# Stick-breaking attention, key block by key block with both heads of a pair side by side

## What is computed

```python
q, k, v, gate = jnp.split(h @ w_in, 4, axis=-1)
q = rms_norm(q.reshape(Bn, T, 16, 64), q_norm_g)
k = rms_norm(k.reshape(Bn, T, 16, 64), k_norm_g)
...
z = jnp.einsum('bqhd,bshd->bhqs', q_blk, k) * scale
mask = key_pos[None, :] < q_pos[:, None]
log1m = jnp.where(mask, -softplus(z), 0.0)
after = cumsum(log1m, axis=3, reverse=True) - log1m
wts = jnp.where(mask, exp(log_sigmoid(z) + after), 0.0)
o = jnp.einsum('bhqs,bshd->bqhd', wts, v)
...
return (o * silu(gate)) @ w_out
```

## Time and profile of the kernel before

| | us |
|---|---|
| time, median of 3 runs (2142.62 to 2148.38) | 2144.33 |
| span of the profiled execution | 2145.8 |
| stick-breaking pairs in it, first `z` to the projection of the gate | 730.3 to 974.9 |

### The profile page before, as it was taken

One profiled execution on the slowest core, in us unless ns is written; L12 is line 12 of the kernel. 1 busy time (PEld: TensorE's weight loads), 2 busy tenths in 40 slices (PEclk: granted clock), 3 DMA queues, 4 the chain that ended last, 5 costly groups with the idle time before them and its releaser, 6 DMA issues.

```text
span 2145.8 us, 28611 instructions
## 1 busy us (share of the span) xinstructions
PE 2056.1 (96%) x10624; PEld 1679.0 (78%) x10624; DVE 1039.1 (48%) x1426; ACT 809.6 (38%) x1169; POOL 619.7 (29%) x156
## 2 busy tenths in 40 slices
PE   6999899999998999999999999999899999999999
PEld 4777788887888766657878888888687788887787
DVE  7856655545424134442564343422874655554620
ACT  5223232237523366563432222222423322234831
POOL 3434000004443210112434444444343300001342
PEclk9999999999999999999999999999999999999999
DMA  4222000002222110111222222222222200000222
GB/s 164 93 98 79 20 1 0 0 0 83 95 98 99 59 40 20 39 39 51 89 96 98 98 95 91 93 92 98 99 98 79 79 1 0 0 0 21 97 98 79
DMA packets 20371, 138.36 MB, mean 64 GB/s; under 512 B 2256, under 2 KB 2384, under 8 KB 4176
## 3 DMA queue, kind: packets, MB, share of 16 engines
q1 hardware_dynamic: 20304, 137.45, 18.2%
HBM read 135.35 MB, written 2.10 MB: 64 GB/s over the span
## 4 chain that ended last, share of the span: by engine, by line
PE 90%; DVE 6%; issue 2%; ACT 1%; POOL 0%; ACTq 0%; DVEq 0%; POOLq 0%
PE ps L1261 20%; PE ps L1263 20%; PE ps L1262 20%; PE ps L1475 4%; PE ps L1459 4%; PE ps L1640 2%; PE ps L1678 2%; PE ps L1666 1%; PE ps L1541 1%; PE ps L1493 1%; PE ps L1522 1%; DVE inv_t L1016 1%; PE ps L1534 1%; PE ps L1523 1%; PE ps L1484 1%
## 5 line engine op out<-in xcount | busy, mean ns | idle before, releaser
L294 POOL TENSOR_TENSOR w_lo<-w_raw,w_hi 128x2048 fp32r<-128x2048 f32 x126 | 589.4, 4678 | 1117.0 <-ACT w_hi L354 1117.0
L1261 PE MATMUL ps<-h_hi,w_hi 128*128 128x512 f32 x1488 | 597.9, 402 | 34.2 <-POOL w_lo L294 20.5
L1262 PE MATMUL ps<-h_lo,w_hi 128*128 128x512 f32 x1488 | 584.1, 393 | 0.0
L1263 PE MATMUL ps<-h_hi,w_lo 128*128 128x512 f32 x1488 | 584.0, 392 | 0.0
L1261 PEld LDWEIGHTS ps<-h_hi,w_hi 128*128 128x128 f32 x1488 | 283.0, 190 | 107.7 <-POOL w_lo L294 21.4
L354 ACT ACTIVATE w_hi<-w_raw 128x2048 fp32r<-128x2048 f32 x126 | 240.4, 1908 | 271.7 <-PE ps L1263 267.2
L1262 PEld LDWEIGHTS ps<-h_lo,w_hi 128*128 128x128 f32 x1488 | 282.8, 190 | 62.3 <-issue 5.1
L1263 PEld LDWEIGHTS ps<-h_hi,w_lo 128*128 128x128 f32 x1488 | 282.1, 190 | 60.1
L1261 PE MATMUL ps<-y_hi,w_hi 128*128 128x512 f32 x448 | 174.3, 389 | 0.0
L1262 PE MATMUL ps<-y_lo,w_hi 128*128 128x512 f32 x448 | 174.3, 389 | 0.0
L1263 PE MATMUL ps<-y_hi,w_lo 128*128 128x512 f32 x448 | 174.3, 389 | 0.0
(11 more groups left out here) (181 smaller groups left out, 2753.1 us busy)
## 6 DMA issues: line engine op xcount, KB each, us to landing
w_raw<-w_tiles SPq DMA_DIRECT2D x126, 1024.0 KB, 4.8
x<-x_t SPq DMA_DIRECT2D x4, 512.0 KB, 7.9
out_t<-x SPq DMA_DIRECT2D x8, 256.0 KB, 5.6
cb<-const_b SPq DMA_DIRECT2D x1, 576.0 KB, 12.0
cf<-const_f SPq DMA_DIRECT2D x1, 352.0 KB, 9.3
par<-params SPq DMA_DIRECT2D x1, 173.0 KB, 2.4
```

The lines of the kernel that those rows point to most:

```text
L294: pool.tensor_tensor(w_lo[:, slot, :], w_raw[:, slot, :], w_hi[:, slot, :].bitcast(F32), ALU.subtract).then_inc(lo_done, 1)
L1261: pe.matmul(out_, w_h, m_h, start=start, stop=False)
L1262: pe.matmul(out_, w_h, m_l, start=False, stop=False)
L1263: return pe.matmul(out_, w_l, m_h, start=False, stop=stop)
```

## The change

The units of a pair are renumbered: kb = 3 - u // 2 and e = u % 2, so that units 2v and 2v + 1 are the two heads at key block 3 - v, with the same width. The pair's loop runs over four steps v.

- TensorE's step v: both `z` one after the other (rows 0 to 63, then 64 to 127), then both masks (now a function of their own, `z_mask`), then both `pv` of two steps before, then 8, 8, 0 and 0 blocks of the next pair's projection, then both `cum` of the step before, and `sums` at v = 2.
- ScalarE's step v: both `softplus`, then both `weights` of the step before; at v = 2 the squares and `rms_qk` follow.
- VectorE's step v: both `softplus`; after those of v = 1 `raws` and then `evac`, after those of v = 2 `scaled`. The wait on `cum` before a unit overwrites `sb_sp` is now for that head's last `cum` of the pair before.
- The waits' counts are refitted to the order. The number of instructions, their shapes and all buffers stay. After the last pair, the tail has `pv(60)` and `pv(61)` before `cum(62)`.

```diff
--- before.py
+++ after.py
@@ -618,7 +618,7 @@
             def softplus(u, j, i):
 
                 n = 8 * j + u
-                kb = 3 - u % 4
+                kb = 3 - u // 2
                 w = T - P * kb
                 zb, tt = ps[2 + u % 4][:, 0:w], sb_t[:, u % 2, 0:w]
                 act.wait_ge(b["z"], n + 1 + 16 * i)
@@ -648,13 +648,14 @@
 
                 t = t0 + 4 + j
                 hi(t + 2, i)
-                for u in range(8):
-                    softplus(u, j, i)
-                    if not (first and u < 2):
-                        weights(8 * j + u - 2, i)
-                    if u == 4 and not last:
+                for v in range(4):
+                    softplus(2 * v, j, i)
+                    softplus(2 * v + 1, j, i)
+                    if not (first and v < 1):
+                        weights(8 * j + 2 * v - 2, i)
+                        weights(8 * j + 2 * v - 1, i)
+                    if v == 2 and not last:
                         square_qk(t + 1, j + 1, i)
-                    if u == 5 and not last:
                         rms_qk(j + 1, i)
 
             pair(0, 0, True, False)
@@ -1123,22 +1124,22 @@
 
             def softplus(u, j, i):
                 n = 8 * j + u
-                kb = 3 - u % 4
+                kb, e = 3 - u // 2, u % 2
                 w = T - P * kb
-                off = (0, 128, 384, 768)[u % 4]
+                off = (0, 128, 384, 768)[u // 2]
                 dve.wait_ge(b["ln1"], n + 1 + 16 * i)
                 if not (isinstance(i, int) and n < 8):
 
-                    dve.wait_ge(b["cum"], 8 * j + 4 * (u // 4) - 4 + 16 * i)
-                dve.scalar_tensor_tensor(sb_sp[:, u // 4, off:off + w], ps[2 + u % 4][:, 0:w], 0.0,
+                    dve.wait_ge(b["cum"], 8 * j - 1 + e + 16 * i)
+                dve.scalar_tensor_tensor(sb_sp[:, e, off:off + w], ps[2 + u % 4][:, 0:w], 0.0,
                                          sb_t[:, u % 2, 0:w], ALU.max, ALU.add).then_inc(b["sp"], 1)
                 if kb < 3:
-                    m = 6 * j + 3 * (u // 4) + u % 4 - 1
-                    own, to = sb_sp[:, u // 4, off:off + w], slice(off - P, off - P + w)
+                    m = 6 * j + u - 2
+                    own, to = sb_sp[:, e, off:off + w], slice(off - P, off - P + w)
                     dve.wait_ge(b["sp"], n + 1 + 16 * i)
-                    dve.tensor_copy(sp_hi[:, u // 4, to], own).then_inc(b["sph"], 1)
+                    dve.tensor_copy(sp_hi[:, e, to], own).then_inc(b["sph"], 1)
                     dve.wait_ge(b["sph"], m + 1 + 12 * i)
-                    dve.tensor_tensor(sp_lo[:, u // 4, to], own, sp_hi[:, u // 4, to].bitcast(F32), ALU.subtract)\
+                    dve.tensor_tensor(sp_lo[:, e, to], own, sp_hi[:, e, to].bitcast(F32), ALU.subtract)\
                         .then_inc(b["spl"], 1)
 
             dve.wait_ge(proj_free, 2 * (t0 + 4))
@@ -1153,13 +1154,14 @@
 
             def pair(j, i, first, last):
                 t = t0 + 4 + j
-                for u in range(8):
-                    softplus(u, j, i)
-                    if u == 3 and not last:
+                for v in range(4):
+                    softplus(2 * v, j, i)
+                    softplus(2 * v + 1, j, i)
+                    if v == 1 and not last:
                         raws(t + 1, j + 1, i)
-                    if u == 4 and not first:
+                    if v == 1 and not first:
                         evac(j - 1, i)
-                    if u == 5 and not last:
+                    if v == 2 and not last:
                         scaled(j + 1, i)
 
             pair(0, 0, True, False)
@@ -1622,8 +1624,8 @@
             sums(0)
 
             def geometry(u):
-                kb = 3 - u % 4
-                return kb, T - P * kb, u // 4
+                kb = 3 - u // 2
+                return kb, T - P * kb, u % 2
 
             def z(u, j, i):
 
@@ -1639,6 +1641,10 @@
                     pe.wait_ge(b["w"], n - 3 + 16 * i)
                 pe.matmul(bk[:, 0:w], sb_qk[rr, j % 2, 1, kb * P:kb * P + P], sb_qk[rr, j % 2, 0, qs],
                           start=True, stop=False, skip_group_check=True)
+
+            def z_mask(u):
+
+                bk = ps[2 + u % 4]
                 pe.matmul(bk[:, 0:P], cb[:, B_ID:B_ID + P], cb[:, B_STRICT:B_STRICT + P],
                           start=False, stop=True, skip_group_check=True).then_inc(b["z"], 1)
 
@@ -1653,7 +1659,7 @@
                 else:
                     if isinstance(i, int) and n == 1:
                         pe.wait_ge(b["tri"], 1)
-                    pe.wait_ge(b["spl"], 6 * (n // 8) + 3 * e + u % 4 + 12 * i)
+                    pe.wait_ge(b["spl"], 6 * (n // 8) + u - 1 + 12 * i)
                 for kb2 in range(kb, NB):
                     w2 = T - P * kb2
                     off = (0, 128, 384, 768)[3 - kb2]
@@ -1680,24 +1686,28 @@
                     .then_inc(b["pv"], 1)
 
             parts = [(c, k) for c in range(2) for k in range(KD)]
-            share = [4, 4, 4, 4]
+            share = [8, 8, 0, 0]
 
             def pair(j, i, first, last):
                 t = t0 + 4 + j
                 rest = list(parts)
-                for u in range(8):
-                    z(u, j, i)
+                for v in range(4):
+                    for e in range(2):
+                        z(2 * v + e, j, i)
+                    for e in range(2):
+                        z_mask(2 * v + e)
+                    if not (first and v < 2):
+                        for e in range(2):
+                            pv(8 * j + 2 * v - 4 + e, i)
                     if not last:
-                        if u == 0:
+                        if v == 0:
                             qk_ready(t + 1, i)
-                        if u < len(share):
-                            for _ in range(share[u]):
-                                qk_part(t + 1, i, *rest.pop(0))
-                    if not (first and u < 2):
-                        cum(8 * j + u - 2, i)
-                    if not (first and u < 3):
-                        pv(8 * j + u - 3, i)
-                    if u == 5 and not last:
+                        for _ in range(share[v]):
+                            qk_part(t + 1, i, *rest.pop(0))
+                    if not (first and v < 1):
+                        for e in range(2):
+                            cum(8 * j + 2 * v - 2 + e, i)
+                    if v == 2 and not last:
                         sums(j + 1, i)
 
             pair(0, 0, True, False)
@@ -1705,8 +1715,9 @@
                 pair(1, i, False, False)
                 pair(2, i, False, False)
             pair(7, 0, False, True)
+            pv(60, 0)
+            pv(61, 0)
             cum(62, 0)
-            pv(61, 0)
             cum(63, 0)
             pv(62, 0)
             pv(63, 0)
```

## The result

The changed kernel takes 2165.88 us (median of 4 runs, 2162.48 to 2167.64) against 2145.71 for the kernel before on the same chip: a ratio of 1.0087, 95% interval 1.0071 to 1.0103, or 19 us slower. The forecast was 27 us slower, within 2149 to 2186. The span went from 2145.8 to 2165.8 us.

What follows compares the result with a forecast made beforehand. TensorE's own work was taken to bound each pair; 28.0 us of it plus 5.4 of waits gave +13 us, clock falls +14, so 2144.3 + 27 = 2171 us, range 2149 to 2186.

Steps and rivals of the forecast that it cites:

- a quarter of overlap: `z` and `pv` at 256 to 512 columns: three matmul lengths in place of four, 1.8 us a pair saved.
- The fourth rival: Full overlap of two heads' products: TensorE's work 27.2, pair 32.6 us, +7 without falls, +18 with; 2151 to 2162; chance 0.10.
- rival 1: No overlap, the tiles' matmuls run one after the other: pair 34.9 us, +24 over the stage, +36 with falls, 2180; chance 0.22.
- TensorE's own work: TensorE's sum per pair: 31.4 less 1.6 net without overlap, less 1.8 from overlap, gives 28.0 us.
- 1.4 + 1.8: `z` and `pv` per pair: 1.4 us of fixed parts the second head doesn't pay, 1.8 us of overlapped streaming.
- The waits: TensorE idle per pair: 2.8 us at `sums`, 1.6 at the next pair's first `z`, three smaller; together 5.4 us.
- the small ones: TensorE waits: 0.5 us at the first step with 256 columns, where `z` follows `cum`, and 0.2 each at two other places.
- +13: Stage loss without clock falls: pairs of 33.4 us, 2.0 more; six full pairs and two ends, 6 x 2.06 + 0.4 us.
- The clock: Pair loop: eight falls to half clock for 3.4 us, 1.7 us of work lost each, +14 us; bounds 0 and 22.
- Rival 2: The clock holds in most pairs: +13 with a quarter of overlap, fewer than four falls, 2151 to 2163, set 2157; chance 0.18.
- the twelve stretches of up to 1.70: TensorE idle stretches of 0.75 to 1.70 us in the trace of before, none of which had a clock fall.
- Rival 3: Faster: ScalarE reaches the squares within 1.7 us of step 2's second mask, TensorE stays full, 24 us less, 2120; chance 0.10.

Runs made afterwards that it cites:

- the run that fills both: Changed kernel with twelve unneeded matmuls ahead of each `sums` and eight at the end of each step 3, in TensorE's two long idle stretches; ratio 1.0016 to the kernel before.
- the squares early: Changed kernel with ScalarE's two squares of the next pair at the end of step 1, ahead of step 2's softplus chains; ratio 1.0013 to the kernel before.
- `z` apart: Changed kernel with each `z` followed by its own mask, so the two heads' `z` can't overlap; `pv` stays in twos; ratio 1.0021 to the kernel before.
- the last version: Kernel before with the new numbering, one unit at a time, four blocks in each of units 0 to 3, only `pv` in twos; ratio 0.9908, 2126.29 us.
- the filling before `sums`: Changed kernel with twelve unneeded bf16 matmuls of 512 columns on TensorE ahead of each `sums`; ratio 1.0059 to the kernel before.
- 6, 5, 5 blocks: Changed kernel with the projection spread as 6, 5, 5, 0 blocks and `raws` behind step 2's `softplus` on VectorE; ratio 0.9975 to the kernel before.
- `pv` apart: Changed kernel with a mask between the two `pv` of a step, so they can't overlap; `z` stays in twos; ratio 1.0090 to the kernel before.
- both edits: Changed kernel with squares at the end of ScalarE's step 1 and each `z` followed by its own mask; ratio 0.9969 to the kernel before.

## Why the prediction was right, and where not

**The bound.** TensorE was the bound, and the listing of the three engines' orders was a usable tool: 31.4 for the pair before. For the pair after it gave 33.4 with a quarter of overlap, and 32.1 was measured where the clock holds.

**The overlap was mis-sized.** I took 1.8 us a pair of at most 3.8, on the ground that a product's two matmuls leave in order. Measured, where both heads can start together, their matmuls cost what one head's do: `pv` of 128 columns 0.37 us against 0.36 (the prediction had counted no overlap at 128), `z` of 512 columns 1.07 against 1.06. So for `pv` the whole half is there: its matmuls take 2.75 us a pair, from start to start, against 5.46 before. `z` takes 4.25 against 5.89, because the second head waits for its own exponential at 128 and 256 columns and starts late at 384. The prediction named this wait and took too little for it. The fourth rival had the overlap right in kind, and rival 1 is out. The Trainium skill (TensorEngine Tiling (Array Packing), Key Properties) says that different tiles can multiply in parallel; the rows after agree for `pv` and for the `z` of 512 columns.

**TensorE's own work** is 27.2 us in the short pair (rows above), against 28.0 in the forecast. `z` and `pv` together saved 4.35 us, where the forecast had 1.4 + 1.8 = 3.2; all the rest saved nothing (20.1 before, 20.2 after), where it had 0.2. The fourth rival's 27.2 is the figure measured, but by luck: with the full half the forecast's own terms give 31.4 - 1.6 - 3.8 = 26.0, a pair of 31.4, and so nothing lost without falls and 11 us with its falls, not +18. That its 2162 lies nearest of all the cases to the 2165.9 measured is luck for the same reason.

**The waits came where they were put.** `sums` 2.8 forecast, 2.70 measured, behind ScalarE's chains at 384 columns; the next pair's first `z` 1.6 forecast, 1.96 measured with the full clock and 1.7 after a fall. Of the small ones, that of 0.5 is the second head's wait at 256 columns, and most of it shows as lost overlap (the 0.54 before the weight loads at 843.90). All idle time of the matmuls in the short pair is 4.9 us, the forecast's waits were 5.4. But what the waits cost over the savings was too high: +13 in the forecast, about 3 in the run that fills both. A pair without a fall was put at 33.4 us and took 32.1: 0.8 of that is TensorE's own work and 0.5 the waits. And the two ends of the stage were put 0.4 us longer and got 1.6 shorter (in the run that fills both).

**The clock** was forecast at +14 with eight falls, and is about 15, but two errors cancel in it. Ten separate stretches at the half clock begin between 733 and 983 us, where before had one, and four of them last 6.8 us and not 3.4: some 48 us at the lower level against 7. Half of the difference is 20 us of work, against the forecast's 8 x 1.7 = 14; only 15 of it came through to the time, where the forecast had all of it come through. So the lower clock lasted longer than forecast, and a quarter of it was hidden. Rival 2 (the clock mostly stays) is out: there was one fall for each pair of the loop on the mean. Two readings in that step were too simple. Of the seven stretches of 2.70 us only four had the fall right behind them, and of those before the next pair's first `z` (1.7 to 2.06 us), which I had counted as harmless by the twelve stretches of up to 1.70, four of seven had one. That there was about one fall a pair comes from the two kinds taking turns, which nothing in the prediction said.

**Rival 3**, faster, failed as it was told: the first square is done 4.4 us after step 2's second mask (819.46 to 823.86), 4.5 in the forecast, and not 1.7. With the squares early and `z` apart the kernel did get faster than before.

So the sign and the mechanism, waits behind ScalarE that also bring the clock down, were right. Of the two terms of the size one was too large (13 for 3), and the other (14 for 15) was met by errors that cancel; the total is 27 for 19.

## What to carry to other kernels

When an order is changed to put work side by side, write down each engine's order and ask which wait has lost the work that lay in front of it; here the reuse of a bank and the squares had lost theirs, and the overlap that was won lay mostly in their shadow. Overlap is worth having only where TensorE's own line is the bound: `pv` in twos gave 2.4 us a pair in the last version, `z` in twos nothing in the changed one. And a loop with idle stretches of TensorE of some 2 us can cost more than these, so that even useless work in it can pay.

## What the runs showed of the hardware

- Two fp32 products in the two halves of the array, by rows (`z`) or by columns (`pv`), run fully beside each other if both may start at once: by rows four matmuls of 512 columns in 1.07 us, two in 1.06; by columns four of 128 columns in 0.37, two in 0.36. A second one that is held up by a wait of its own loses this: four `z` of 128 columns took 0.80 us, two 0.42, and four of 256 columns 1.46 with the wait and 0.63 without.
- Which idle stretch brings TensorE's clock down isn't told by its length alone. In the loop a fall came behind all seven stretches of 2.55 to 2.65 us with the early squares, behind four of seven of 2.70 us in the changed kernel, behind five of seven of 1.95 to 2.06 us with the filling before `sums`, behind one of seven of 1.75 us with `z` apart, behind one of seven of 1.95 to 2.04 us with 6, 5, 5 blocks, and behind none of 2.24 us in the profile with `pv` apart. It even came twice in the loop with both edits, where no stretch is longer than 0.98 us. What else counts is not settled here.
- Where the clock falls in the loop, pairs can alternate (36.3 and 32.1 us; 31.9 and 33.1), though each does the same work, and two kernels spread widely from execution to execution, with the granted clock: `pv` apart from 2156 us at 0.989 to 2174 at 0.982, `z` apart from 2145 at 0.988 to 2158 at 0.984. The kernel before spread from 2143 to 2150 beside them.
